# Leaving out TensorE's filler products between the stages of a two-block transformer kernel

## The reference

```python
def rms_norm(x, g):
    x32 = x.astype(jnp.float32)
    y = x32 * lax.rsqrt(jnp.mean(x32 * x32, axis=-1, keepdims=True) + RMS_EPS)
    return (y * g.astype(jnp.float32)).astype(x.dtype)

def modulate_pre(x, g_pre, shift, scale):
    return rms_norm(x, g_pre) * (1.0 + scale[:, None, :]) + shift[:, None, :]

def gated_post_add(x, y, g_post, gate, weight):
    return x + weight * gate[:, None, :] * rms_norm(y, g_post)

# first block, per layer
mod = (jax.nn.silu(c) @ ada_w[layer] + ada_b[layer]).reshape(B, 3, 3, D)
h = modulate_pre(x, g[0, 0], mod[:, 0, 0], mod[:, 0, 1])
y = swiglu_ffn(h, ffn_w_in[layer, 0], ffn_w_out[layer, 0])
x = gated_post_add(x, y, g[0, 1], mod[:, 0, 2], 0.5)
...
# second block, per layer
h = rms_norm_2(x, norm1[l]) * (1.0 + sc1) + sh1
...
x = x + gt1 * (merged @ w_out[l])
h2 = rms_norm_2(x, norm2[l]) * (1.0 + sc2) + sh2
hidden = jnp.square(jax.nn.relu(h2 @ w_ff1[l]))
x = x + gt2 * (hidden @ w_ff2[l])
```

## Time and profile before

| what | value |
|---|---|
| median of 3 runs | 2412.24 us (2407.43 to 2412.79) |
| span of the profiled execution, first to last instruction | 2399.2 us |
| mean granted TensorE clock over the span | 0.956 |
| TensorE busy | 2315.6 us, 97% |
| VectorE busy | 1532.9 us, 64% |
| ScalarE busy | 973.9 us, 41% |
| GpSimd busy | 142.2 us, 6% |
| moved from memory | 490.69 MB, 205 GB/s |

### The profile page before, as it was taken

The page is one execution under the profiler, slowest core; times in us unless marked ns, Lnnn a source line. Parts: engine busy times, 40 slices in busy tenths (PEclk is TensorE's granted clock), DMA queues, the critical chain, the costliest instruction groups (busy, mean ns, idle before and its releaser), DMA issues.

```text
span 2399.2 us, 43691 instructions
## 1 busy us (share of the span) xinstructions
PE 2315.6 (97%) x18388; PEld 2279.2 (95%) x18388; DVE 1532.9 (64%) x1387; ACT 973.9 (41%) x956; POOL 142.2 (6%) x210
## 2 busy tenths in 40 slices
PE   4999999999999999799999999999999999999998
PEld 4999999999899999589999999999999999999997
DVE  5877568775547765757776444758885435566554
ACT  2443444433423433544334444334443445334442
POOL 1000101110000000010001000001000000000000
PEclk7999999998879997899998999999998999999999
DMA  7988357994549953038964535448983544454552
GB/s 241 368 314 292 106 176 271 318 324 135 174 148 334 319 183 106 1 110 315 320 247 169 171 128 175 159 161 294 336 314 115 176 154 159 146 175 157 178 184 78
DMA packets 256366, 493.64 MB, mean 206 GB/s; under 512 B 16240, under 2 KB 145648, under 8 KB 255984
## 3 DMA queue, kind: packets, MB, share of 16 engines
q1 hardware_dynamic: 231920, 365.96, 45.8%
q0 software_dynamic: 24320, 125.84, 13.6%
HBM read 490.69 MB, written 1.05 MB: 205 GB/s over the span
## 4 chain that ended last, share of the span: by engine, by line
PE 92%; DVE 3%; ACT 2%; DMA 2%; issue 1%; SPq 0%; DVEq 0%; ACTq 0%
PE PA L502 14%; PE PA L504 14%; PE PA L503 14%; PE PY L502 7%; PE PY L504 7%; PE PY L503 7%; PE PB L502 5%; PE PB L503 5%; PE PB L504 5%; PE PB L556 2%; PE PB L545 2%; PE PA L563 2%; DMA adaw<-ada_w 1%; PE PY L836 1%; DVE rstd L1360 1%; ACT acc L1198 1%
## 5 line engine op out<-in xcount | busy, mean ns | idle before, releaser
L1312 DVE TENSOR_TENSOR wlo<-raw,whi 128x2048 fp32r<-128x2048 f32 x335 | 764.7, 2286 | 487.0 <-ACT whi L994 343.9
L502 PE MATMUL PA<-opA_hi,whi 128*128 128x256 f32 x2528 | 719.1, 284 | 1.3 <-DVE opA_lo L1371 1.3
L504 PE MATMUL PA<-opA_hi,wlo 128*128 128x256 f32 x2528 | 717.7, 284 | 0.0
L503 PE MATMUL PA<-opA_lo,whi 128*128 128x256 f32 x2528 | 717.7, 284 | 0.0
L994 ACT ACTIVATE whi<-raw 128x2048 fp32r<-128x2048 f32 x203 | 384.9, 1901 | 305.1 <-PE PA L504 140.0
L502 PEld LDWEIGHTS PA<-opA_hi,whi 128*128 128x128 f32 x2528 | 487.9, 193 | 1.9 <-issue 1.8
L503 PEld LDWEIGHTS PA<-opA_lo,whi 128*128 128x128 f32 x2528 | 487.8, 193 | 0.1
L504 PEld LDWEIGHTS PA<-opA_hi,wlo 128*128 128x128 f32 x2528 | 487.7, 193 | 0.0
L502 PE MATMUL PY<-opB_hi,whi 128*128 128x256 f32 x1344 | 386.1, 287 | 2.2 <-DVE opB_lo L1480 1.5
L503 PE MATMUL PY<-opB_lo,whi 128*128 128x256 f32 x1344 | 384.7, 286 | 0.0
L504 PE MATMUL PY<-opB_hi,wlo 128*128 128x256 f32 x1344 | 384.5, 286 | 0.0
(11 more groups left out here) (245 smaller groups left out, 2891.0 us busy)
## 6 DMA issues: line engine op xcount, KB each, us to landing
raw<-ffn_w_in SPq DMA_DIRECT2D x176, 512.0 KB, 5.2
raw<-w_in SPq DMA_DIRECT2D x144, 512.0 KB, 4.7
raw<-w_ff SPq DMA_DIRECT2D x128, 512.0 KB, 4.4
raw<-ffn_w_out SPq DMA_DIRECT2D x88, 512.0 KB, 4.7
adaw<-ada_w POOLq DMA_DIRECT2D x40, 768.0 KB, 6.3
mix<-ada_w POOLq DMA_DIRECT2D x32, 768.0 KB, 6.2
adaw<-w_ada POOLq DMA_DIRECT2D x32, 768.0 KB, 6.0
mix<-w_ada POOLq DMA_DIRECT2D x32, 768.0 KB, 6.1
```

The lines of the kernel that those rows point to most:

```text
L502: nc.tensor.matmul(o_, w1, rhs(xh), start=start, stop=False, skip_group_check=True)
L503: nc.tensor.matmul(o_, w1, rhs(xl), start=False, stop=False, skip_group_check=True)
L504: return nc.tensor.matmul(o_, w2_, rhs(xh), start=False, stop=stop, skip_group_check=True)
L1312: TT(wlo[slot][:, 0:w], raw[slot][:, 0:w], whi[slot][:, 0:w].bitcast(F32), ALU.subtract).then_inc(lo_ready, 1)
```

## The change

All fillers are left out: those of the first modulation, those in the two gaps of a boundary, and the single ones between the groups of `ssq`. `later` still issues its one-column products where it did. No result depends on a filler.

```diff
-GAP_Y, GAP_X, GAP_B = 22, 16, 5
...
-            def ssq(tag, gap=0):
+            def ssq(tag):
 
                 take("B")
                 for k in range(KT):
                     if k % 2 == 0:
-                        if k:
-                            idle(gap)
                         need(pe, "S", f"{tag}.sq{k // 2}")
...
-            def idle(n):
-
-                for _ in range(n):
-                    nc.tensor.matmul(flat["A"][:, 0:P], ident, onesD, start=True, stop=True)
...
                 if not sub.startswith("b"):
                     ssq_pairs(f"{sub}.y")
-                    idle(GAP_Y - (later(job_, 0) if job_ else 0))
-                    ssq(f"{nsub}.x", 1)
+                    if job_:
+                        later(job_, 0)
+                    ssq(f"{nsub}.x")
                 else:
-                    idle(GAP_B)
                     ssq(f"{nsub}.x")
-                if nsub != "fin":
-                    idle(GAP_X - (later(job_, 1) if job_ else 0))
+                if nsub != "fin" and job_:
+                    later(job_, 1)
 
             pe.wait_ge(base_in, 16)
             ssq("00.x")
-            for k in range(6, KT):
-                pe.wait_ge(ada_used[3], k)
-                idle(10)
             finish_mods("first")
-            idle(14)
             ffn("ffn00", 0, "00")
```

## The result

The kernel without fillers has a median of 2422.49 us (2415.76 to 2424.72, 6 runs) against 2407.37 us (2398.07 to 2412.79, 6 runs) for the kernel before. The ratio is 1.0065 with a 95% interval of 1.0042 to 1.0088: 10 to 21 us slower, 15.7 at the middle. The span of the profiled execution is 2414.1 us, 14.9 above that of before, and its mean granted clock is 0.943 for 0.956. One other execution of the kernel before, among those timed beside the last two experiments, took 9977.61 us; it is left out of every comparison, and its cause isn't known.

The account below looks back on a forecast made before the run. TensorE, busy 97% of the span, was taken as the bound. The terms 0.7 + 8.1 + 13.7 + 1.4 - 3.0 - 3.8 gave +17.1 us on a median of 2412.2: 2429.3 us, range 2416 to 2446.

Parts of the forecast that it names:

- (a): Kernel start: first weight product 0.9 us earlier but then cold, +0.7 us (0 to +1.6).
- (b): First stop, 5.2 us, in six boundaries: second sum of squares runs partly cold, +1.35 us each, +8.1 in all.
- (d): Three boundaries with 24 one-column instructions: cold, these outlast the second stop by 0.9 us in half the cases, +1.4 us.
- (e): Cold stretches already paid in spite of fillers, at 908.5, 1280.78 and 1289.9, credited against double counting: -3.0 us.
- (c): Second stop, 4.2 us, nine boundaries: cold weight products follow, eight times 1.6 and once 0.9, +13.7 us (7.4 to 21.8).
- the forecast's own sign of being wrong: Boundaries with one-column products were so cold before that nothing is added there; the other sign was clock 1.00 through 4.2 us stops.
- (f): Second block, four boundaries: the sum starts earlier without fillers, at full clock, 4 x 0.95 = -3.8 us.
- only the longer stops cost: Rival: clock falls in the 5.2 us stops but holds through 4.2 us; +6.4 us, 2418.6; chance 0.12.
- the clock follows only the kind of product: Rival: stops don't lower the clock, so the kernel gets faster, -8.7 us, 2403.5; chance 0.05.
- Everything cold: Rival: every cold term at its bound, +34.3 us, 2446.5; chance 0.08.
- hidden: Rival: weight products have slack to catch up, so about 0 change; chance 0.05.
- work around the span: The 13.0 us by which the median of 2412.24 exceeded the span of 2399.2, taken as untouched by the edit.

Follow-up runs that it names:

- the last two experiments: Against the kernel before: two long one-column blocks halved with GAP_B 0, ratio 0.9963; and all fillers out except the second stop's, ratio 0.999.
- the last experiment: All fillers left out except those of the second stop (GAP_X, nine boundaries), against the kernel before: 2401.87 us, ratio 0.999 (0.9976 to 1.0005).
- the first (GAP_B): Only the five fillers ahead of the sum in the second block's four boundaries left out, against the kernel before: 2399.83 us, ratio 0.9991.
- the eighth (the long blocks): Against the kernel before: GAP_B 0, and 20 of 40 and 24 of 48 one-column products spread among weight products: 2394.08 us, ratio 0.9963.
- the fifth (the start): Only the fillers of the first modulation (10, 10 and 14) left out, against the kernel before: one run, 2403.07 us.
- the second experiment: Only the fillers after the sum of squares of x (GAP_X, nine boundaries) left out, against the kernel before: 2422.29 us, ratio 1.0073.
- the light fillers: Every filler kept in number and place but with one column in place of 128, against the kernel before: 2444.23 us, ratio 1.0162.

## Why the prediction was right

The direction, the main mechanism and the size came out: +17.1 us foretold, 15.7 measured by the ratio, 14.9 by the two spans. That the sum came so near is in part luck: single terms missed by up to 2.9 us, and the misses cancel. By its steps:

- **(a) start, +0.7.** Measured +1.0 against the profile of before, alone and in the whole change: -0.84 and +1.80. The -0.57 of the table holds 1.5 us of an earlier arrival. But the step took it that the fillers help the one-column products to 4.24 us, and in six other traces with the same fillers these take 5.2 to 7.0. Against most executions leaving them out gains a little, so the sign of this term is open.
- **(b) first stop, 1.35 each.** Up to the first weight product the trace of the change has 2.3, 2.3, 1.4, 0.9 and 0.7 in five boundaries, mean 1.5; with the first stops alone open it is 1.0 each over six, in the last experiment 1.2. The mechanism is shown and 1.35 lies among these values. But all six boundaries of the change, with 12 to b00 at -1.9, add up to 5.8 us, where the sum had 8.1 + 1.4 from (d) - 0.8 from (e) = 8.7. The ratios of the two experiments (1.0013 and 0.999) speak for a few microseconds in all.
- **(c) second stop, 1.6 each, 13.7 in all.** The column "second" has 13.3 in the trace of the change, 13.6 with the second stops alone open, and the ratio of the latter says 17.6 (10.6 to 24.3). These are net of what before pays at the same places; the term to hold beside them is 13.7 - 0.9 - 1.3 from (e) = 11.5, some 2 us less. This term carries the result.
- **(d) one-column products outlasting the second stop, +1.4.** It didn't occur: at 00, 10 and 12 they ran in 2.73 us, warm, and TensorE then stood some 1.45 us until the operand came. The term was 0.
- **(e) cold stretches paid before, -3.0.** At 12 to b00 the change is 1.6 us faster than the profile of before, where I had reckoned with 1.3 slower; this is the forecast's own sign of being wrong, in one of the three boundaries with one-column products. Three experiments leave this boundary as it is, and they don't agree on its price: against the profile of before the first (GAP_B) is 2.7 us quicker in it, the eighth (the long blocks) 0.4 slower, the fifth (the start) 4.3 slower. What before pays here is a draw between 35.0 and 42.0 us, and I took one draw for a fixed cost.
- **(f) second block, -3.8.** Measured -3.6 in the change (0.71, 1.11, 0.70, 1.11), -3.65 alone.

The mean granted clock fell by 0.013, where about 0.02 was foretold, and groups of the sum near 1.7 us stand at 01 to 02 but not in all six boundaries: the sums of the changed kernel last 5.1 to 6.7 us, partly warm.

The rival that only the longer stops cost is the wrong way round: the shorter second stop costs more (1.0073 against 1.0013). That this is because dense work stands behind it, and only a sum and fillers behind the first, is an argument and not a measurement. The rival that the clock follows only the kind of product fell with the 4.0 us stops in the second experiment; its other half is true, as the light fillers show: kind and stops both count. *Everything cold* and *hidden* fell with 15.7 us (10 to 21).

The 109 ns that the prediction sets against its 120 stands in the Trainium skill (TensorE: Matmul & The Clock Gate, section Back-to-back issue gap) as the gap of an isolated product. For a stream of weight loads and products the same section says that both set the spacing, and it names no figure for 256 columns, so the 120 ns measured here doesn't contradict it.

The forecast of 2429 was 6.5 us above the measured median. 4.9 of that is the base: the median of the kernel before was 2412.24 in three runs and 2407.37 in six. The 13.0 us that I called work around the span was no such thing: the changed kernel's profiled execution took 2415.76 us with a span of 2414.1, so 1.7 lies around, and by the same distance the profile of before belongs to an execution of some 2401 us, quicker than the three timed ones.

## What to carry to other kernels

Read the granted clock behind each stop and each run of small products, not the busy share; price a stop as the length of the cold stretch behind it times 0.44, the loss per microsecond for this kernel's weight products. Look for that stretch past the stop as well: here it began up to 1.1 us after work had resumed. Fill a stop only where it would really stand open, up to the moment when the next operand is there: fillers ahead of work that is ready are delay (five per boundary here, 3.7 us), and half a fill still left 0.45% of 0.73%. Read a place in several executions before calling its cost fixed: one trace of before misled the forecast at the start and at 12 to b00. Before moving small products out of a block, look for the wait that the block covers.

## What the runs showed of the hardware

- One-column products let the clock fall at full occupation of TensorE (1.00 to 0.53, with products busy 3.90 of 3.90 us and weight loads 3.72).
- The clock can fall after a stop is over: 1.1 us of products at 1.00 after a stop of 4.0 us, then 3.3 us at 0.50.
- A stop of 2.24 us with 1.95 us of fillers ahead of it was enough for such a fall.
- At the lower level an instruction of a float32 product of 256 columns takes 0.43 us (14 in 5.98 us, kernel after at 373.00), for 0.22 warm (16 in the 3.53 us from 1626.88 to 1630.41, first experiment): close to twice. A weight product takes 213 ns for 120, 1.8 times.
- Executions of one and the same kernel spread over 0.7%, and one boundary (12 to b00) took 35.0, 37.7, 38.1 and 42.0 us in four executions in which nothing there had changed.
